# A one-core hybrid DeltaNet and Hyena trunk: three seams between its stages rearranged together

## The chip, the cores and the metric

The kernel runs on one core of one Trainium2 chip. The time is that of the whole program on the device, in microseconds. TensorE is called PE, its weight load PEld, VectorE DVE, ScalarE ACT, GpSimd POOL and SyncE SP.

## The reference

One layer over a sequence of 2048 tokens of width 1024, and 256 context tokens:

```python
mod_x = silu(c) @ w_mod + b_mod                      # shift, scale and gate, each 1024 wide
hx = rmsnorm(x, norm_g) * (1.0 + sc_x) + sh_x
px = hx @ w_in                                       # q, k, v, z_a, betas, decays, hy_v, hy_x1, hy_x2, z_b, g_a, g_b
ox, _ = deltanet(px, lp, rows, GRID_W, ctx_states)   # chunked gated delta rule, forward and backward, 8 heads
yx = hyena(px, lp, rows, GRID_W)                     # two long convolutions by Fourier transform
x = x + gt_x * ((sigmoid(g_a) * (ox @ w_pa) + sigmoid(g_b) * (yx @ w_pb)) @ w_out)
out = rmsnorm(x, final_g)
```

The sum of the two delta directions is normed per head (mean of squares of 128 values) before it is gated and multiplied by `w_pa`. All is fp32.

## The kernel before

Five stages run one after the other, each in a block of its own: `modulate`, `project`, `delta`, `hyena`, `merge`. Each stage has a `Kit` that holds its on-chip buffers and semaphores. At its end all engines meet at a barrier and the semaphores are cleared (L159), so a stage's last DMA that must have landed holds back the next stage. Two outer kits, `shared` and `tail`, keep what several stages use. Within a stage each engine has its own written order of instructions, and waits on counting semaphores. SP issues most DMAs, POOL some from a queue of its own, ACT a few.

**modulate.** A tile is 128 tokens of 1024 values; there are 18, the first two context. POOL loads a tile into one of four slots `xin`; ACT squares and sums it (`square`), DVE makes the mean, ACT the root, DVE inverts and scales it into `xs`, PE turns it in eight transposes (`tile`), and ACT and DVE move half each out of PSUM (`move`). Between tiles PE multiplies the condition by `w_mod`, in 12 pieces of 256 columns (`piece`), of which the first 8 (shift and scale) are needed before anything can be shaped, and the last 4 are the gate row. The slots `wm` of the first 8 pieces lie in `hB`, where the last eight tiles go. So `HEAD_TILES` (10) tiles run first with a piece each, then the windows 0 (context), 1 and 2 are shaped (`shape`: scale and shift), then the other eight tiles with the gate's pieces through one buffer `wmg`, then windows 3 and 4. A window of the sequence is 512 tokens. The sums S1 to S4 are operands of a seven-product scheme in `project`: those of the first half of the sequence are made between the last eight tiles, those of the second half after the last shaping, and all seven operands of the second half are stored to `comb` by SP, which `modulate` waits for. `gate_products` multiplies each shaped window by the 32 columns of betas and decays, `keep` copies them out, `gate_turns` turns them. POOL loads the first two blocks of `w_in` into `wt` after 15 tiles.

**project.** 40 steps, each a pair of 128-column blocks of `w_in` for one half of the sequence, in seven products (P1 to P7). SP's queue stores the results to scratch tensors: `store(s - 2, 1)` and `store(s - 1, 0)` in turn `s`.

**delta.** 72 pairs of heads. For each, SP loads `rows`, `kq`, `nv`, `ttc` and `tnc` for both directions, ten DMAs, into a ring of `DEPTH` = 6; `sc` holds all scalars. POOL subtracts (`differences`, L1704) and places blocks (L1713), ACT takes exponentials, DVE weighs, PE multiplies (L1939, L1882, and others).

**hyena.** Eight steps `t` (four blocks of channels, two orders). In each, PE, ACT and DVE make spectra and products, and SP stores the eight parts of the inverse to `bounce_i` (L2172), waits for all, and reads them back turned (L2178); PE then makes the eight output banks `O` (L2521), and DVE empties them (`outputs`). In the last step this is followed by turning the result to channels (`results`), and by the store of `yT` (L2183), for which the stage waits. POOL's queue also loads what the merge needs: its weights `w_pb` and rows in `merge_weights`, and in `merge_operands` `w_pa` (4 MB, L2331) when the last T bank is filled and the delta's `o` (two loads of 1 MB, L2335) when the last M bank is.

**merge.** Eight windows of 256 tokens. In each, POOL adds the directions of `o` (L2781), ACT squares, DVE reduces, inverts and scales, per half (`norm_half`); PE turns `o` (L2898), DVE weighs with `z_a` (L2840). Behind it, for the window before, come eight products of `w_pa` and `w_pb` (L2908, L2912), DVE's gates (L2850), POOL's mix (L2790), `w_out` (L2926) and the final norm. The engines' order per window puts both `norm_half` ahead of the gates on DVE.

## Time and profile before

| | |
|---|---|
| Runs | 4446.98 us median of 3 (4445.2 to 4453.29) |
| The profiled execution | 4446.54 us, its span 4444.8 us |
| Busy share | PE 95%, DVE 55%, POOL 39%, ACT 28% |
| Mean granted TensorE clock | 0.974 |
| HBM traffic | 405 MB read, 218 MB written, 140 GB/s over the span |

Times in the rows are microseconds from the span's start. A row of the timeline gives the start and the length of a run of like instructions, the engine (SPq is SP's queue of DMA issues), the source line, output and inputs, the number of instructions, and in brackets how long the engine had been idle before it and what ended that.

### The profile page before, as it was taken

What the parts mean: (1) busy time and instruction counts of PE and PEld (TensorE: products, weight loads), DVE (VectorE), ACT (ScalarE), POOL (GpSimd) and SP (SyncE); (2) the same over time, 40 slices, a digit from 0 to 9 for tenths busy, and PEclk for the clock granted to TensorE, in tenths of its full rate; (3) what the DMA queues carried; (4) which work ended last, traced back from release to release, by engine and by line L of the source; (5) the groups of instructions that cost most, each with busy time, mean ns of one, the idle gap of its engine ahead of it and who ended that gap; (6) DMA issues with size and microseconds to landing.
All of it is one profiled execution on the core that took longest, in us unless ns stands there. A gap on an engine that the chain in (4) does not pass through costs nothing. (4 is left out here: it accounts for less than half of the span.)

```text
span 4444.8 us, 72318 instructions
## 1 busy us (share of the span) xinstructions
PE 4225.1 (95%) x28915; PEld 2587.0 (58%) x28915; DVE 2437.7 (55%) x3482; ACT 1233.2 (28%) x2592; POOL 1752.8 (39%) x1487
## 2 busy tenths in 40 slices
PE   5899999999999999999979999989999996999998
PEld 3466544444445544444437888856565654767776
DVE  4555755542446668896616666657676763222221
ACT  4122121111222211111115555555555551000000
POOL 1222233332333343433339989845444451111111
PEclk7999999999999999999989999999999997999999
DMA  6323222223242342425337788567767677223320
GB/s 232 103 74 98 76 94 82 76 95 115 82 154 85 107 117 81 123 76 166 108 128 210 217 261 248 165 178 229 223 195 230 213 246 273 76 76 115 111 76 29
DMA packets 481064, 627.05 MB, mean 141 GB/s; under 512 B 120928, under 2 KB 379944, under 8 KB 470124
## 3 DMA queue, kind: packets, MB, share of 16 engines
q1 hardware_dynamic: 431596, 484.22, 35.9%
q0 software_dynamic: 28560, 113.25, 7.9%
q10 hardware_dynamic: 20592, 25.16, 1.7%
q8 instruction: 222, 3.64, 0.3%
q14 instruction: 94, 0.77, 0.1%
HBM read 405.01 MB, written 217.53 MB: 140 GB/s over the span
## 5 line engine op out<-in xcount | busy, mean ns | idle before, releaser
L1458 PE MATMUL proj_b<-shared_S,proj_tw 128*128 128x512 f32 x1920 | 850.8, 595 | 0.0
L1458 PEld LDWEIGHTS proj_b<-shared_S,proj_tw 128*128 128x128 f32 x1920 | 361.7, 191 | 433.9 <-issue 433.5
L1458 PE MATMUL proj_b<-shared_A,shared_wt 128*128 128x512 f32 x1280 | 577.4, 594 | 13.0 <-PEq L159 12.3
L820 POOL TENSOR_TENSOR proj_tw<-shared_wt 128x512 f32<-128x512 f32 x80 | 109.9, 1374 | 921.3 <-PE proj_b L1458 838.6
L1458 PEld LDWEIGHTS proj_b<-shared_A,shared_wt 128*128 128x128 f32 x1280 | 243.8, 191 | 317.5 <-issue 317.1
L1458 PE MATMUL proj_b<-shared_A,proj_tw 128*128 128x512 f32 x640 | 289.4, 595 | 3.2 <-DVE proj_u L1125 3.2
L1458 PE MATMUL proj_b<-shared_S,shared_wt 128*128 128x512 f32 x640 | 290.9, 597 | 0.0
L1023 ACT ACTIVATE proj_v<-proj_b 128x512 f32<-128x512 f32 x80 | 47.8, 597 | 634.9 <-PE proj_b L1458 634.9
L1840 DVE SCALAR_TENSOR_TENSOR delta_la<-delta_kkq,delta_sc,delta_wm 128x256 f32<-128x256 f32 (+1 forms) x288 | 121.6, 464 | 173.3 <-PE delta_kkq L1939 173.2
L1458 PEld LDWEIGHTS proj_b<-shared_A,proj_tw 128*128 128x128 f32 x640 | 122.2, 191 | 157.6 <-issue 152.6
L1704 POOL TENSOR_SCALAR delta_ex<-delta_rows,delta_sc 128x128 f32<-128x128 f32 x288 | 203.5, 721 | 22.5 <-DMA delta_tnc<-scratch_Tn 22.5
L1120 DVE TENSOR_TENSOR proj_u<-proj_b,proj_u 128x512 f32<-128x512 f32 x80 | 55.2, 690 | 277.0 <-PE proj_b L1458 276.8
L2926 PE MATMUL mrg_b<-mrg_w_o,tail_u 128*128 128x512 f32 x448 | 198.3, 594 | 6.7 <-POOL tail_u L2790 4.3
L834 POOL TENSOR_TENSOR proj_tw<-shared_wt,proj_tw 128x512 f32<-128x512 f32 x80 | 116.7, 1458 | 199.9 <-PE proj_b L1458 199.8
L1719 POOL TENSOR_SCALAR delta_kg<-delta_nv,delta_sc 128x128 f32<-128x128 f32 x288 | 187.9, 668 | 10.1 <-PE delta_kv L1956 10.1
L1136 DVE TENSOR_TENSOR proj_rawx<-proj_b,proj_u 128x512 f32<-128x512 f32 x144 | 97.5, 683 | 172.0 <-PE proj_b L1458 171.9
L1458 PEld LDWEIGHTS proj_b<-shared_S,shared_wt 128*128 128x128 f32 x640 | 117.1, 191 | 128.2 <-issue 127.8
L1014 ACT ACTIVATE proj_u<-proj_b 128x512 f32<-128x512 f32 x80 | 47.6, 596 | 517.0 <-PE proj_b L1458 494.7
L2416 DVE TENSOR_TENSOR fft_second<-fft_b,fft_second 128x512 f32<-128x512 f32 x256 | 159.5, 682 | 54.6 <-PE fft_b L2544 47.1
L2310 POOL TENSOR_TENSOR tail_u<-tail_u,fft_ga 128x4096 f32<-128x4096 f32 x8 | 71.5, 8935 | 266.7 <-DMA fft_ga<-scratch_hy 137.9
L844 POOL TENSOR_TENSOR proj_u<-proj_u,proj_v 128x512 f32<-128x512 f32 x80 | 136.0, 1700 | 103.0 <-ACT proj_v L1023 102.9
L806 POOL DMA_DIRECT2D shared_wt<-in_w_in_dram x78 | 70.5, 904 | 265.2 <-PE proj_b L1458 265.2
(333 smaller groups left out, 8583.1 us busy)
## 6 DMA issues: line engine op xcount, KB each, us to landing
shared_wt<-in_w_in_dram POOLq DMA_DIRECT2D x80, 1024.0 KB, 6.0
delta_nv<-scratch_NV SPq DMA_DIRECT2D x144, 256.0 KB, 4.1
delta_kq<-scratch_KQ SPq DMA_DIRECT2D x128, 256.0 KB, 4.3
scratch_bounce_f<-tail_first SPq DMA_DIRECT2D x128, 256.0 KB, 4.4
tail_yf<-scratch_bounce_f SPq DMA_DIRECT2D x32, 1024.0 KB, 7.3
scratch_bounce_i<-fft_yi SPq DMA_DIRECT2D x64, 512.0 KB, 3.4
fft_second<-scratch_bounce_i SPq DMA_DIRECT2D x32, 1024.0 KB, 8.6
scratch_hy<-proj_tok SPq DMA_DIRECT2D x48, 512.0 KB, 2.6
```

The costliest lines, as they stand in the source:

```text
L806: pool.dma_start(wt[:, s % 2, :, :], wv[:, :, col:col + 2 * P]).then_inc(w_in[s % 2], 16)
L820: pool.tensor_tensor(T3, w[:, hi, second], w[:, lo, second], ALU.subtract).then_inc(combined, 1)
L834: pool.tensor_tensor(T4, w[:, hi, first], T2, ALU.subtract).then_inc(combined, 1)
L844: pool.tensor_tensor(u4[:, :], u2[:, :], v5[:, :], ALU.add).then_inc(fourth, 1)
L1136: dve.tensor_tensor(out, rows(bank[:, :]), rows(addend[:, :]), ALU.add).then_inc(dve_read, 1)
L1458: last = pe.matmul(bank[:, :], weights[:, k, :], aa[operand][:, k, :], start=(k == 0), stop=(k == KH - 1))
L1704: last = pool.tensor_scalar(ex[:, n % 2, d, g, :], rows[:, n % DEPTH, d, g, :], scalar(n, d, g, Q_NGC), 0.0, ALU.add, ALU.min)
L1719: last = pool.tensor_scalar(kg[:, n % SYS, d, g, :], nv[:, n % DEPTH, d, g, 0, :], scalar(n, d, g, Q_BKL), None, ALU.mult)
L1840: last = dve.scalar_tensor_tensor(out=la[:, n % SYS, d, g, parts, :], in0=b_kkq[g][:, 2 * P * d:2 * P * (d + 1)].rearrange("p (a t) -> p a ...
L2310: pool.tensor_tensor(data, data, ga[:, :, :, :], ALU.mult).then_inc(gated, 1)
L2416: dve.tensor_tensor(dst[h % 2][:, i, :], bank(kind, t, 2 * h + i)[:, :], xs[h % 2][:, i, :], ALU.mult).then_inc(emptied["dve"], 1)
L2926: last = pe.matmul(out_banks(h)[b][:, :], mt[:, k, h * P:(h + 1) * P], w_o(k)[:, 512 * b:512 * b + 512], start=(k == 0), stop=(k == KT - 1))
```

## The change

It has three parts, joined by one shared space.

**A shared space.** A new outer kit, `bridge`, keeps a region of 7360 values per partition and three semaphores through the whole program. `modulate` puts its short-lived buffers there, `project` its scratch region, `delta` its scalars and the first two of the six ring entries, and `hyena` and `merge` their `yf` and `hs`.

**modulate.** `wm` now lies over S1 to S4, the four gate pieces have a buffer each, and all 18 tiles run first, with a piece at every second one. After that all five windows are shaped in a row; of windows 3 and 4 ACT shapes five rows of eight and DVE three. The sums of the first half stand between windows 2 and 3, in one group. `keep` comes after all shaping, and POOL loads `wt` after all tiles.

**delta's operands ahead.** SP loads `sc2` and the first two pairs in the last step but one turn of `project`, before it stores that turn's results. `delta` waits for these at its start, SP goes on with pair 2, the clearing of the state moves from POOL to DVE, and ACT makes one exponential at once.

**The merge's first norm.** In the hyena's last step POOL loads `o` first, adds both halves, and loads `w_pa` after output bank 1 is filled. ACT and DVE make the norm of window 0 before the last outputs; `epsq` and `dng` are loaded for it by SP. The wait for the store of `yT` moves from the hyena's end to the merge, before SP's load of `yb`.

The diff, cut to its core:

```diff
+        wm = [aa[x][:, :, :].rearrange("p k t -> p (k t)").rearrange("p (k n) -> p k n", k=KT) for x in ("S1", "S2", "S3", "S4")]
+        wg = [wmg[:, :, :], pieces(xin[:, 2:4, :]), pieces(xin[:, 0:2, :]), pieces(xs[:, :, :])]
+        def split(w):
+            return KH if w < HEAD else KH - 1
...
+                sp.dma_start(wg[0], gates[:, 0, :, :]).then_inc(wg_in[0], 16)
+                sp.wait_ge(scaled, NCH - 2)
+                sp.dma_start(wg[1], gates[:, 1, :, :]).then_inc(wg_in[1], 16)
+                sp.wait_ge(scaled, NCH)
+                sp.dma_start(wg[2], gates[:, 2, :, :]).then_inc(wg_in[2], 16)
+                sp.wait_ge(turned, NCH)
+                sp.dma_start(wg[3], gates[:, 3, :, :]).then_inc(wg_in[3], 16)
...
-                    if i == NCH - NX:
-                        for s in range(2):
+                pool.wait_ge(products, HEAD_PIECES)
+                for s in range(2):
...
-                tiles(0, HEAD_TILES)
-                for w in range(HEAD):
+                tiles(0, NCH)
+                for w in range(5):
                     shape(w)
-                for w in range(2):
-                    keep(w)
-                tiles(HEAD_TILES, NCH)
-                for w in range(HEAD, 5):
-                    shape(w)
-                for w in range(2, 5):
+                for w in range(5):
                     keep(w)
...
+                def sums(w):
+                    for who in ("act", "dve"):
+                        dve.wait_ge(shaped[who], w)
+                    if w > HEAD:
+                        dve.wait_ge(summed, 3)
+                        dve.wait_ge(differed, 1)
+                        dve.wait_ge(z_done, 3)
...
+                tiles(0, NCH, keep_vectors)
                 vectors()
                 for w in range(HEAD):
                     shape(w)
-                tiles(HEAD_TILES, NCH, sums)
+                sums(3)
                 for w in range(HEAD, 5):
                     shape(w)
...
+                sums(5)
...
-                for i in range(HEAD_TILES):
+                for i in range(NCH):
                     tile(i)
-                    if i >= 4 and i % 2 == 0:
-                        vectors(i // 2 - 2)
-                    if i >= 2:
-                        piece(i - 2)
+                    if i >= 6 and i % 4 == 2:
+                        vectors(i // 4 - 1)
+                    if i >= 2 and i % 2 == 1:
+                        piece(i // 2 - 1)
...
+def load_pair(sp, T, ring, n, landed):
+    chunks, j = pair_of(n)
+    for d in range(2):
+        c, heads = chunks[d], slice(2 * j, 2 * j + 2)
+        parts = slice(0, parts_of(n))
...
+                def pairs_ahead():
+                    last = first_step(1, "k") + H // 2 - 1
+                    sp.wait_ge(inv_out, 64 * NPIECE)
+                    sp.wait_ge(sc_out, 48)
+                    for m in range(2):
+                        sp.wait_ge(tok_out[m], 16 * tok_dmas[NSTEP])
+                        for s in (last - 1, last):
+                            sp.wait_ge(chan_out[s % 2][m], 16 * chan_stores(s))
+                    sp.dma_start(S["bridge"][:, 0:SC_SIZE], T["sc2"].rearrange("p c h d q -> p (c h d q)")).then_inc(S["sc_in"], 16)
+                    for n in range(AHEAD):
+                        load_pair(sp, T, ring_entry(S["bridge"], SC_SIZE + n * RING_SIZE), n, S["pair_in"][n])
                 for s in range(NSTEP + 2):
+                    if s == NSTEP - 1:
+                        pairs_ahead()
                     store(s - 2, 1)
...
-                sp.dma_start(sc[:, :, :, :, :], T["sc2"]).then_inc(loaded, 16)
                 sp.dma_start(tri[:, :, :], T["tri"]).then_inc(loaded, 16)
                 sp.dma_start(blocks[:, :], T["blocks"]).then_inc(loaded, 16)
-                sp.wait_ge(cleared, 1)
-                for n in range(NPAIR):
-                    chunks, j = pair_of(n)
+                for n in range(AHEAD, NPAIR):
...
-                pool.memset(S[:, :, :, :], 0.0).then_inc(cleared, 1)
-                pool.wait_ge(loaded, 48)
+                pool.wait_ge(L["sc_in"], 16)
...
+                act.activation(warm[:, :], sc[:, 0, 0, 0, 0:1], ACT.Exp, scale=0.0)
...
+                dve.memset(S[:, :, :, :], 0.0).then_inc(cleared, 1)
...
+                    if t == STEPS - 1:
+                        epsq, _, _, dng = tail_norm(L)
+                        sp.dma_start(epsq, T["epsq"]).then_inc(L["small"], 16)
...
-                sp.dma_start(T["yT"][2 * NCB - 2:2 * NCB, :, :].rearrange("h p t -> p h t"), yt).then_inc(y_stored, 16)
-                sp.wait_ge(y_stored, 16 * NCB)
+                sp.dma_start(T["yT"][2 * NCB - 2:2 * NCB, :, :].rearrange("h p t -> p h t"), yt).then_inc(L["y_out"], 16)
...
-                    ready(pool, "T", last, N2 - 1)
-                    pool.dma_start(tail_w_a(L), T["w_pa"][0].rearrange("(k p) n -> p k n", p=P)).then_inc(L["w_a_in"], 16)
                     ready(pool, "M", last, N2 - 1)
...
+                    o = tail_o(L)
+                    pool.wait_ge(L["o_in"], 32)
+                    for h in range(2):
+                        pool.tensor_tensor(o[:, h, 0, :], o[:, h, 0, :], o[:, h, 1, :], ALU.add).then_inc(L["summed"], 1)
+                    ready(pool, "O", last, 1)
+                    pool.dma_start(tail_w_a(L), T["w_pa"][0].rearrange("(k p) n -> p k n", p=P)).then_inc(L["w_a_in"], 16)
...
+                def first_norms():
+                    o, (epsq, ms, sd, _) = tail_o(L), tail_norm(L)
...
+                    for h in range(2):
+                        dve.wait_ge(L["rooted"], h + 1)
+                        dve.reciprocal(sd[:, h, :], sd[:, h, :]).then_inc(L["inverted"], 1)
+                        dve.wait_ge(L["inverted"], h + 1)
+                        dve.tensor_tensor(heads(o[:, h, 0, :]), heads(o[:, h, 0, :]), sd[:, h, :].unsqueeze(2).broadcast_to([P, H, P]), ALU.mult).then_inc(L["scaled"], 1)
                 for t in range(STEPS + 1):
+                    if t == STEPS:
+                        first_norms()
...
+                        if off == 0:
+                            sp.wait_ge(L["y_out"], 16)
...
+        B = {"bridge": kit.sb("region", P, SC_SIZE + AHEAD * RING_SIZE), "sc_in": kit.sem("sc_in"), "pair_in": [kit.sem(f"pair_in{n}") for n in range(AHEAD)]}
```

## Rows read from the trace of the kernel before

**Rows 1.** The page, part 1: busy time of each engine.
```profile
PE 4225.1 (95%) x28915; PEld 2587.0 (58%) x28915; DVE 2437.7 (55%) x3482; ACT 1233.2 (28%) x2592; POOL 1752.8 (39%) x1487
```

**Rows 2.** Windows: length, busy us (instructions) of each engine, granted clock, DMA share, GB/s.
```profile
4.00:48.00 44.00, 27.45 (x227) 19.37 (x230) 19.01 (x49) 19.25 (x42) 5.71 (x10) 0.92 1.07 369
3678.00:3697.00 19.00, 1.45 (x24) 0.18 (x16) 0.32 (x1) 1.08 (x2) 0.63 (x1) 0.63 0.98 380
```

**Rows 3.** Timeline of the first 130 us.
```profile
47.51 1.58 PE L485 MATMUL mod_b<-mod_hB,mod_scond 128*32 128x256 f32 x16 [2.42 <-DMA mod_hB<-in_w_mod_dram]
...
52.35 2.07 ACT L330 ACTIVATE shared_hc<-mod_hA,mod_mod,mod_gsc 128x256 f32<-128x256 f32 x4 [6.62 <-DVE mod_gsc L413]
...
54.33 5.74 ACT L330 ACTIVATE shared_A<-mod_hA,mod_mod,mod_gsc 128x512 f32<-128x512 f32 x8
...
55.47 1.91 DVE L423 TENSOR_SCALAR mod_hA<-mod_hA,mod_gsc,mod_mod 128x512 f32<-128x512 f32 x4
...
60.48 3.64 PE L516 MATMUL mod_b<-shared_A,mod_wbg 128*32 128x512 f32 x16 [4.06 <-ACT mod_zs L337]
...
106.16 2.76 SPq L268 DMA_DIRECT2D scratch_comb<-mod_hB  x3
...
112.90 2.29 DVE L456 TENSOR_TENSOR mod_hA<-mod_hB,mod_hA 128x2048 f32<-128x2048 f32 x1
...
129.46 5.56 PE L1458 MATMUL proj_b<-shared_A,shared_wt 128*128 128x512 f32 x8 [12.30 <-PEq L159]
```

**Rows 4.** Timeline of the seam between projection and delta.
```profile
2307.69 1.80 POOL L1697 MEMSET delta_S<- 128x2048 f32 x1 [14.01 <-POOLq L159]
...
2309.52 0.33 SPq L1688 DMA_DIRECT2D delta_rows<-scratch_gcT  x1
...
2314.70 0.47 SPq L1688 DMA_DIRECT2D delta_rows<-scratch_gcT  x1
...
2318.24 2.80 POOL L1704 TENSOR_SCALAR delta_ex<-delta_rows,delta_sc 128x128 f32<-128x128 f32 x4 [8.74 <-DMA delta_tnc<-scratch_Tn]
```

**Rows 5.** Timeline of the hyena's last gap.
```profile
3675.35 0.95 POOL L2331 DMA_DIRECT2D tail_first<-in_w_pa_dram  x1
...
3677.23 1.41 POOL L2335 DMA_DIRECT2D tail_yf<-scratch_o  x2 [0.93 <-PE fft_b L2544]
...
3696.78 2.04 SPq L2178 DMA_DIRECT2D fft_second<-scratch_bounce_i  x4
3701.60 16.74 PE L2521 MATMUL fft_b<-fft_second,tail_ia 128*128 128x256 f32 x64 [22.14 <-DMA fft_second<-scratch_bounce_i]
3705.49 0.69 DVE L2396 TENSOR_TENSOR fft_ga<-fft_b,fft_ga 128x512 f32<-128x512 f32 x1 [27.18 <-PE fft_b L2521]
...
3724.74 0.39 SPq L2183 DMA_DIRECT2D scratch_yT<-fft_ga  x1
```

**Rows 6.** Tile `fft_yi`, 3640 to 3700: landing of its eight bounce stores.
```profile
DMA to landing us min/median/max: 2.9/3.8/16.0
```

**Rows 7.** Timeline of the merge's start.
```profile
3732.74 4.64 POOL L2781 TENSOR_TENSOR tail_yf<-tail_yf 128x1024 f32<-128x1024 f32 x2 [54.10 <-SPq L2709]
...
3733.72 0.38 SPq L2728 DMA_DIRECT2D tail_ia<-scratch_yT  x1
...
3739.66 1.94 PE L2898 MATMUL mrg_b<-tail_ident,tail_yf 128*128 128x128 f32 x8 [16.09 <-DVE tail_yf L2828]
...
3747.51 5.62 PE L2908 MATMUL mrg_b<-tail_aT,tail_first 128*128 128x256 f32 x16 [1.59 <-DVE tail_aT L2840]
...
3769.07 2.06 DVE L2850 TENSOR_TENSOR mrg_gg<-mrg_b,mrg_gg 128x512 f32<-128x512 f32 x3
...
3778.01 3.62 PE L2908 MATMUL mrg_b<-tail_aT,tail_first 128*128 128x256 f32 x16
```

**Rows 8.** `scratch_yT`, 3700 to 3735: landing of the store (6.4) and of `yb` (5.4).
```profile
DMA to landing us min/median/max: 5.4/5.9/6.4
```

**Rows 9.** Timeline of the end.
```profile
4439.35 0.39 SPq L2740 DMA_DIRECT2D out_dram<-tail_u  x1
```

More of the change, by code:

```diff
@@ L1601 @@
 SYS = 3
-def pair_of(n):
-    s, j = divmod(n, PAIRS)
-    back = NCTX - 1 - s if s < NCTX else NCH - 1 - (s - NCTX)
-    return (s, back), j
 def level_blocks(d, h):
@@ L1641, in delta @@
         loaded, cleared = kit.sem("loaded"), kit.sem("cleared")
-        landed = [kit.sem(f"landed{i}") for i in range(DEPTH)]
+        landed = [L["pair_in"][i] if i < AHEAD else kit.sem(f"landed{i}") for i in range(DEPTH)]
         stored = [kit.sem(f"stored{i}") for i in range(2)]
@@ L2674, in merge @@
         ident = L["ident"]
-        dng, eps = kit.sb("dng", P, 1), kit.sb("eps", P, 1)
-        epsq = kit.sb("epsq", P, NCH, H)
+        epsq, _, _, dng = tail_norm(L)
+        eps = kit.sb("eps", P, 1)
         ms, sd, rs = (kit.sb(n, P, 2, H) for n in ("ms", "sd", "rs"))
@@ L2710, in _ @@
                 sp.sem_inc(za_in[0], 16)
-                sp.dma_start(epsq[:, :, :], T["epsq"]).then_inc(small, 16)
-                with nc.allow_non_contiguous_dma(reason="a vector into a column"):
-                    sp.dma_start(dng[:, :], T["dn_norm_g"][0].rearrange("(p a) -> p a", a=1)).then_inc(small, 16)
                 sp.sem_inc(stored, 16)
@@ L2816, in norm_half @@
                     def norm_half(h):
-                        if not front:
+                        if not front or off == 0:
                             return
```

228 lines of the change are left out of this document (131 added, 97 removed).

## The prediction

> **What bounds the kernel now.** I read the page first. TensorE is busy 95% of the span [rows 1], so time can come back only from the 5% in which it idles. Then I asked for the windows of 100 to 500 us over the whole span: the idle time stands in three places, the first 129 us, the seam of projection and delta near 2305 us, and the stretch from 3680 to 3750 us, the last gap of the hyena and the start of the merge. For each I took the timeline in order of time, the waits, and the windows with the DMA rate. The change touches exactly these three.
>
> In the first place the transfers are saturated, not the engines: from 4 to 48 us they moved 369 GB/s while PE was busy 27 of 44 us [rows 2]. At the second seam nothing computes while the first pair's loads are issued and land: POOL is free at 2307.69 (its first work is a memset) and its first subtraction starts at 2318.24 [rows 4]. In the third, DMA moved 380 GB/s for 19 us while PE was busy 1.45 of them [rows 2]: `w_pa`, `o` and the last bounce store drain together, 7.3 MB, and only then does SP read the bounce back at 3696.78 [rows 5]. After that come the wait for the store of `yT` and a norm before PE turns anything.
>
> **Front.** Removed: the split of the 18 tiles into 10 and 8 with the shaping of three windows between them. All tiles now come first, a piece of `w_mod` with every second one, from four slots laid over S1 to S4. The bytes needed before the last tile and piece: 18 tiles of 0.52 MB, 8 pieces of 1.05 MB, and one gate piece and `wbg` queued beside them, 19.0 MB. At 369 GB/s [rows 2] from 4 us on that is 51.5 us, so 55.5. Before, from the last piece's products (47.51) to the first shaping (52.35) were 4.8 us [rows 3]; so shaping starts at 60, called T. Per tile the transfers need 2.8 us. The engines need less: for the ten tiles before, ACT was busy 19.3 us and PE, pieces included, 27.5 [rows 2], so DMA paces it. If handshakes do (before, a tile with its piece took 4.35 us; let one without still need 3.4, an estimate between this and the 2.8), T is 4 + 61.2 + 4.8 = 70; with the gate piece not in the way, T is 57. I take 60, since the row at 369 GB/s is the nearest.
>
> From T: ACT shapes window 0 (2.07 for four) and windows 1 and 2 (5.74 for eight) [rows 3], to T+7.8; DVE is quicker, 1.91 for four. Then DVE's four sums of 2.28 each [rows 3], to T+17.1, and its three rows of windows 3 and 4, 6 x 0.48, to T+20.0. ACT has ten of 0.72 there and is done at T+15. Then the seven stores to `comb` begin, as at 106.16 before, and the projection begins 23.3 us later, at 129.46 [rows 3], because the stores' 7.3 MB and the closing of the block take that long. Late next: the copies `keep` now stand behind all shaping on ACT, and the second sums wait for the third gate product. That product comes at about T+24 (two of 3.64 us at the low clock [rows 3] and their copies), so the sums end 3.5 us later, at T+32.6. The first three stores alone fill the DMA until T+28 and S1 and S3 until T+34, so this is hidden; without that cover it costs 3.5. The projection starts at T+43.3 = 103.3, for 129.46: **-26.1** (bounds -16 and -29). The loads of `wt` move behind all tile loads on POOL's queue and land by about T+10, free; DMA idles from there to T+20.
>
> **Projection to delta.** SP issues `sc2` and two pairs (21 DMAs) in step 39's turn. A pair takes 5.2 us of SP's queue (2309.52 to 2314.70 [rows 4]), so 10.9 us. Behind them wait the last stores of `gb`, whose buffers are needed two steps on; 40 steps fill 129.46 to 2307.69, 54 us each in the mean, so I count nothing; uncovered it is 10.9. At the seam POOL's subtraction may start at once at 2307.7 instead of 2318.24: **-10.5**. The memset goes to DVE (POOL's took 1.80 [rows 4]; from half to twice that there, an estimate), behind DVE's two others, and is hidden until about 2311.2, when POOL's four subtractions (2.80 [rows 4]) and the exponential behind them are done. `tri` and `blocks` are now the first loads; if they land as late as pair 0's last (some 4 us from its issue, 2318.24 less 2314.2), POOL's placements move from 2310.5 to 2312.4, which costs up to 1.9. Against that ACT's table load is made ahead. Pair 2 is issued from 2308.6 instead of 2314.70, 6 us earlier, while POOL wants it 10.5 earlier, about 2320; with landing it is there by 2318. I take -10.0, bounds -8 and -12.
>
> **Last gap and merge.** (a) `w_pa`, 4.2 MB, leaves the queue at 3675.35 and is issued only after the second output bank. What remains at 3677.8 is `o` (2.1 MB) and two bounce stores (1.05 MB): 3.15 MB at 380 GB/s [rows 2] is 8.3 us, so 3686 instead of 3696.78 [rows 5]: I take 3685.5, as other stores there landed in 2.9 to 3.8 us and only this one in 16.0 [rows 6]. PE's outputs begin 11.3 us earlier, at 3690.3 (bounds: 12.4 if the store lands at once in 3.8, 0 if something else holds it). `w_pa` goes out at 3697.2, behind POOL's adds, beside the end of the read-back and needs 11 us at that rate; PE asks for it at 3715.4.
>
> The Trainium skill ("DMA: Bandwidth & Descriptors", section "Queues, rings and completion order") says that a DMA engine takes turns between the queue rows it has work for, packet by packet. With equal shares of bytes the store would last at most twice 3.8 us whatever the other queue holds, also in the changed kernel, and the gap would shrink by 8.7 instead of 11.3; the 16.0 of [rows 6] shows that the shares are not equal here, so the trace decides.
>
> (b) The norm in the gap: `o` is there at 3686, POOL adds two halves (4.64 us [rows 7] for both), ACT squares, DVE reduces, inverts and scales. In the merge the first half took 3732.74 to 3739.66 [rows 7], 6.9 us; the second ends some 3.5 behind it: about 10.4 us, to 3696.4. DVE's first output bank is full at 3705.49 - 11.3 = 3694.2, so DVE is 2.2 us late. It needs 1.4 us a bank (two instructions of 0.69) where PE brings one in 2.1 in the mean (16.74 for eight) [rows 5], so it has caught up before the last. Cost 0 (up to 3 if `o` lands late). `epsq` and `dng` on SP fall into an idle stretch.
>
> (c) The `yT` store goes out at 3724.74 - 11.3 = 3713.4; the hyena no longer waits for its 6.4 us [rows 8]. Before, the merge began 8.0 us after the issue [rows 5, 7], so now 1.6 after it plus the issue: 3715.4. PE turns and DVE weighs, twice: 7.85 us before, from 3739.66 to 3747.51 [rows 7], of which some 0.7 waited for the second half's norm; with 7.1 the first product could start at 3722.5 instead of 3747.51. (d) But what is late next is SP: it waits for the store's landing, 3719.8, before it issues `yb`, `gg`, `w_out` and the next window's `o`. That queue set the next norm: from the issue of `yb`, 3733.72, to DVE's first gate, ending at 3769.8, are 36.0 us, DMA-bound, and the fifth product (3778.01) had 8 us to spare [rows 7]. Now the gate ends at 3719.8 + 36.0 = 3755.8, while PE would have been ready at 3722.5 + 30.5 = 3753.0: it waits 2.8 us. The fifth product starts at 3755.9 for 3778.01: **-22.1**, whatever clock PE has on the way. `yb` itself lands after 5.4 us [rows 8], in time.
>
> **End.** One more kit is closed. From the last store's issue at 4439.35 to 4444.8 [rows 9] are 5.4 us with a landing and two closings; one closing after the 6.4 us of `yT` took 1.6. **+0.7** (0 to 1.6).
>
> **Sum.** -26.1 - 10.0 - 22.1 + 0.7 = -57.5. Against the profiled execution's 4446.5 that is 4389.0; the runs' median is 0.4 higher, which I leave.
>
> **Rivals.**
> *The front is paced by handshakes*, not bytes: T = 70, the projection at 113, 4399. For it: 4.35 us a tile is near the bytes' own 4.25, so the row does not show how short the chain can be; against: no engine was busy two thirds of the time. 20%.
> *The last gap does not shrink*, because the store is held by `o` or by packet sharing: 11.3 are lost, 4400. For it: `o` stays in the gap; against: its bytes are a third. This is also the case in which moving `w_pa` does not do what it says. 14%.
> *`w_pa` comes late*: at the pace of a 0.5 MB store (3.8 us [rows 6]) 4 MB take 30 us, PE waits from 3715.4 to 3727, and of this 8.8 stay after (d): 4398. For it: nothing shows that transfer alone; against: the same queue was the largest part of 380 GB/s. 6%.
> *More comes back*: T = 57 (3), the delta at its bound (2), the store at once (1), the merge's loads 2 us quicker: 4381. 10%.
> *Slower*: TensorE's granted clock. It averaged 0.974. If the denser schedule made the clock fall there, each hundredth costs some 42 us of the 4225 busy ones [rows 1]; from 1.4 hundredths on the kernel is slower, 4456 at 1.6. Nothing in the trace hints at it: gaps lower the clock here (0.63 in the gap [rows 2]), work does not. 2%.
>
> **Numbers.** My own case, 4382 to 4396, 48%. The range runs from the bound "more" to beyond the front and the gap rivals: 4376 to 4406; outside it are both rivals at once and the slow one. A change of under 0.2%, 9 us, cannot be told from none; faster 0.97, same 0.01, slower 0.02.
>
> **What would show it.** The first product of the projection at 103 (a step of 3 tells T). POOL's first subtraction in the delta within a microsecond of its start. The read-back of the bounce 6 to 7 us after the last store instead of 16. PE's turn right at the start of the merge, then one wait of about 3 us for a gate before the fifth product. Wrong would be: DMA below 350 GB/s in the first 50 us, the gap still 22 us, or a PE wait for `w_pa` at the merge's start.

## The result, and the profile after

The changed kernel takes 4398.44 us (median of 4 runs, 4395.3 to 4402.8), the kernel before 4447.57 (4 runs). The ratio is 0.9893, with a 95% interval of 0.9881 to 0.9906: faster by 49 us where 57.5 were forecast, inside the range of 4376 to 4406. The profiled execution has a span of 4396.3 us for 4444.8, so 48.5 less. TensorE's mean granted clock is 0.980 for 0.974.

The two traces, cut at landmarks that both have:

| stretch | before | after | difference | forecast |
|---|---|---|---|---|
| start to the projection's first product | 129.46 | 110.44 | -19.0 | -26.1 |
| to DVE's first memset of the delta | 2178.4 | 2177.3 | -1.1 | 0 |
| to POOL's first subtraction | 10.4 | -0.35 | -10.7 | -10.0 |
| to the hyena's last inverse bank (TensorE, 16 products in a row) | 1359.0 | 1357.2 | -1.8 | 0 |
| to the issue of the last `yT` store | 47.5 | 39.4 | -8.1 | -11.3 |
| to the fifth product of the merge | 53.3 | 43.3 | -10.0 | -10.8 |
| to the end | 666.8 | 669.0 | +2.2 | +0.7 |

The stretches that the change leaves alone also differ between executions. Over the 12 kernels below, the projection's ran from 2173.9 to 2180.1 us, the fourth from 1354.4 to 1364.0 and the last from 667.2 to 669.1. A single execution therefore says nothing about a whole time within 5 us or so, and the experiments are read by stretch.

The page of the changed kernel, part 1, against [rows 1]:
```profile
PE 4219.2 (96%) x28915; PEld 2583.1 (59%) x28915; DVE 2441.7 (56%) x3481; ACT 1234.5 (28%) x2595; POOL 1750.6 (40%) x1486
```
TensorE does the same work in 5.9 us less busy time; the other 42.6 us were idle time.

Timeline of the front, changed kernel, against [rows 3]: the issues of two late tiles, the arrival of the last (its square on ACT), the last piece's products, the first shaping, the first store of `comb`, the projection:
```profile
40.09 0.53 POOL L297 DMA_DIRECT2D mod_xin<-in_x_dram  x1 [4.65 <-DVE bridge_region L384]
...
50.01 0.53 POOL L297 DMA_DIRECT2D mod_xin<-in_x_dram  x1 [1.20 <-DVE bridge_region L384]
...
58.20 1.06 ACT L313 ACTIVATE bridge_region<-mod_xin 128x1024 f32<-128x1024 f32 x1 [0.54 <-DMA mod_xin<-in_x_dram]
...
63.91 1.07 PE L481 MATMUL mod_b<-shared_S,mod_scond 128*32 128x256 f32 x16
...
67.46 2.07 ACT L339 ACTIVATE shared_hc<-mod_hA,mod_mod,mod_gsc 128x256 f32<-128x256 f32 x4 [2.84 <-DVE mod_gsc L415]
...
87.05 2.75 SPq L279 DMA_DIRECT2D scratch_comb<-mod_hB  x3
...
110.44 2.05 PE L1506 MATMUL proj_b<-shared_A,shared_wt 128*128 128x512 f32 x2 [10.80 <-PEq L159]
```
T is 67.5 and not 60; from T on the stores start 19.6 later (20.0 was forecast) and the projection 43.0 later (43.3). The bracket on the POOL rows is the point: POOL had the next load ready and waited for DVE to be done with the slot. Windows of the same stretch:
```profile
4.00:24.00 20.00, 8.28 (x37) 6.79 (x41) 8.28 (x26) 10.47 (x23) 2.99 (x5) 1.00 1.06 373
24.00:44.00 20.00, 14.85 (x122) 10.07 (x115) 10.92 (x27) 11.67 (x28) 3.26 (x7) 0.85 1.00 353
...
40.00:44.00 4.00, 4.00 (x26) 2.40 (x27) 2.31 (x6) 2.15 (x7) 1.06 (x2) 0.50 0.88 294
44.00:48.00 4.00, 3.97 (x40) 3.15 (x38) 2.96 (x9) 2.71 (x6) 0.53 (x1) 0.90 0.82 278
```
The last column falls from 373 and 353 GB/s to 294 and 278 between 40 and 48 us, where TensorE is full, for four of these us at a granted clock of 0.50, its lower level of 1.2 GHz. There the transfers wait for the engines; in the next 8 us they are back at 327 and 388 GB/s.

Timeline of the second seam, against [rows 4]:
```profile
2287.43 2.80 POOL L1733 TENSOR_SCALAR delta_ex<-bridge_region 128x128 f32<-128x128 f32 x4 [14.13 <-POOLq L159]
...
2288.86 1.30 PE L1974 MATMUL delta_kkq<-bridge_region 128*32 128x128 f32 x32 [7.75 <-DVE delta_kkq L1851]
2289.22 1.76 DVE L1852 MEMSET delta_S<- 128x2048 f32 x1 [0.42 <-issue]
...
2293.54 0.44 PE L1915 MATMUL delta_lev<-bridge_region,delta_la 32*32 32x32 f32 x16 [3.38 <-DVE delta_la L1874]
```
The subtraction starts with the block instead of 10.4 us into it, and `delta_lev` follows it by 6.1 us for 6.9 before. The memset of `S` lies beside POOL's subtractions, as counted.

Timeline of the last gap and the merge's start, against [rows 5, 7]:
```profile
3637.55 10.87 SPq L2212 DMA_DIRECT2D scratch_bounce_i<-fft_yi  x4
...
3644.61 1.48 POOL L2383 DMA_DIRECT2D bridge_region<-scratch_o  x2 [3.15 <-PE fft_b L2615]
...
3654.54 4.64 POOL L2387 TENSOR_TENSOR bridge_region<-bridge_region 128x1024 f32<-128x1024 f32 x2 [8.45 <-DMA bridge_region<-scratch_o]
3656.08 1.97 SPq L2218 DMA_DIRECT2D fft_second<-scratch_bounce_i  x4
...
3684.06 0.39 SPq L2223 DMA_DIRECT2D scratch_yT<-fft_ga  x1
3685.86 0.06 DVE L2887 MEMSET mrg_eps<- 128x1 f32 x1 [1.87 <-PEq L159]
3686.89 1.94 PE L2985 MATMUL mrg_b<-tail_ident,bridge_region 128*128 128x128 f32 x8 [4.00 <-DVEq L2893]
...
3691.22 0.38 SPq L2806 DMA_DIRECT2D tail_ia<-scratch_yT  x1
...
3694.12 5.14 PE L2995 MATMUL mrg_b<-tail_aT,tail_first 128*128 128x256 f32 x16 [1.58 <-DVE tail_aT L2925]
...
3727.32 5.41 PE L2995 MATMUL mrg_b<-tail_aT,tail_first 128*128 128x256 f32 x16 [2.71 <-DVE mrg_gg L2935]
```
The last of the four stores goes out at the end of its row, at 3648.05, and the read-back 8.0 us behind it, for 16.1 before and 4.8 forecast. `o` is there at 3654.5: the store, issued behind it, lands behind it. The last row shows the forecast wait before the fifth product, 2.7 us for 2.8.

### The profile page after: what moved, and what is told of

Same layout as the page of the kernel before. It is cut to its first block and busy times, and to the rows that moved or that the text cites. A ratio compares the mean times of both kernels' runs of the same rounds, so it can differ in the third digit from the quotient of the medians.

```text
span 4396.3 us, 72326 instructions
## 1 busy us (share of the span) xinstructions
PE 4219.2 (96%) x28915; PEld 2583.1 (59%) x28915; DVE 2441.7 (56%) x3481; ACT 1234.5 (28%) x2595; POOL 1750.6 (40%) x1486
## 3 DMA queue, kind: packets, MB, share of 16 engines
q1 hardware_dynamic: 431596, 484.22, 36.4%
## 5 line engine op out<-in xcount | busy, mean ns | idle before, releaser
L1506 PE MATMUL proj_b<-shared_A,shared_wt 128*128 128x512 f32 x1280 | 578.5, 595 | 11.4 <-PEq L159 10.8
L1874 DVE SCALAR_TENSOR_TENSOR delta_la<-delta_kkq,bridge_region,delta_wm 128x256 f32<-128x256 f32 (+1 forms) x288 | 121.5, 463 | 170.7 <-PE delta_kkq L1974 170.5
L2353 POOL TENSOR_TENSOR fft_acc<-fft_acc,fft_yi 128x512 f32<-128x512 f32 x120 | 153.1, 1276 | 38.3 <-ACT fft_yi L2257 27.7
L2841 ACT ACTIVATE tail_fan<-tail_u 128x1024 f32<-128x1024 f32 x16 | 16.9, 1057 | 530.5 <-POOL tail_u L2882 530.5
```

What stands on the lines that cost most here:

```text
L1506: last = pe.matmul(bank[:, :], weights[:, k, :], aa[operand][:, k, :], start=(k == 0), stop=(k == KH - 1))
L1874: last = dve.scalar_tensor_tensor(out=la[:, n % SYS, d, g, parts, :], in0=b_kkq[g][:, 2 * P * d:2 * P * (d + 1)].rearrange("p (a t) -> p a ...
L2353: pool.tensor_tensor(acc[:, :], acc[:, :], sq[:, n % 2, :], ALU.add).then_inc(added, 1)
```

## Experiments

All are edits of the changed kernel. T is the start of the shaping, "behind the last bank" counts from the last inverse bank of the hyena.

**Front: what sets T.** Three kernels.

e1, each piece a tile earlier on TensorE:
```diff
-                    if i >= 2 and i % 2 == 1:
+                    if i >= 2 and i % 2 == 0:
                         piece(i // 2 - 1)
-                    q, rest = divmod(n - 7, 4)
+                    q, rest = divmod(n - 6, 4)
```


> The changed kernel with each of the first eight pieces multiplied one tile earlier (the last one stands between the last two tiles on TensorE instead of behind the last). Theory A, the time T at which shaping starts is the landing of the last tile (58.2) plus the chain behind it, 9.3 us, in which the last piece's products are a link of 1.9 us: T falls from 67.5 to about 65.6 and the projection starts at 108.5 instead of 110.4; the whole about 2 us shorter. Rival B, the last piece waits for its own transfer or for the handshakes of the tiles, so its place on TensorE changes nothing: T stays at 67.5 within 0.5. DMA up to 56 us is the same in both.

e2, six slots:
```diff
-        NX, NW = 4, 4
+        NX, NW = 6, 4
+        spare = aa["A22"][:, :, :].rearrange("p k t -> p (k t)")
+        x_slot = lambda i: xin[:, i % NX, :] if i % NX < 4 else spare[:, (i % NX - 4) * D:(i % NX - 3) * D]
...
-                    pool.dma_start(xin[:, i % NX, :], source(i))
+                    pool.dma_start(x_slot(i), source(i))
```


> The changed kernel with six slots for the tiles of x instead of four (the two more lie in an operand that is free until the shaping). Theory B, the slots pace the front (a tile's load is issued only when the tile four before it is scaled): the last issue moves from 50.0 to about 44, DMA holds 370 GB/s from 40 to 52 us instead of 278 to 330, the 19.0 MB are in by 55.4, and T falls by 2.5 us or more, to 65 or less. Theory A, the bytes pace it as they are: the loads are issued earlier but land at the same times, T stays between 66.5 and 67.5.

e3, the gate piece behind the tiles:
```diff
-                sp.dma_start(wg[0], gates[:, 0, :, :]).then_inc(wg_in[0], 16)
                 sp.wait_ge(scaled, NCH - 2)
+                sp.dma_start(wg[0], gates[:, 0, :, :]).then_inc(wg_in[0], 16)
```


> The changed kernel with the first gate piece (1.05 MB) issued only when sixteen tiles are scaled, so behind the tiles instead of among them. Theory A, bytes: the last tiles land 1.05 MB / 370 GB/s = 2.8 us earlier and T falls to about 64.7, the projection starts 2.8 us earlier. Theory B, slots and handshakes: T stays at 67.5 within 0.5.

| | last tile issued | squared | last piece | T | square to T |
|---|---|---|---|---|---|
| changed kernel | 50.0 | 58.2 | 63.9 | 67.5 | 9.3 |
| e1 | 52.8 | 58.5 | 61.8 | 65.3 | 6.9 |
| e2 | 40.3 | 51.1 | 55.8 | 59.4 | 8.3 |
| e3 | 49.8 | 57.3 | 63.6 | 67.2 | 9.9 |

The eight other kernels here that have this front unchanged up to T (e4 to e11) put T at 66.0 to 69.0, and the last square at 57.5 to 59.2. e2 lies far outside: T falls by 8.1 us, and 7.1 of them are the last tile's earlier square. Its timeline and windows:
```profile
40.31 0.53 POOL L299 DMA_DIRECT2D shared_A<-in_x_dram  x1 [5.79 <-DVE bridge_region L386]
...
59.39 2.07 ACT L341 ACTIVATE shared_hc<-mod_hA,mod_mod,mod_gsc 128x256 f32<-128x256 f32 x4 [2.84 <-DVE mod_gsc L417]
...
102.44 6.08 PE L1508 MATMUL proj_b<-shared_A,shared_wt 128*128 128x512 f32 x8 [9.76 <-PEq L159]
```
```profile
24.00:44.00 20.00, 14.62 (x120) 10.77 (x116) 12.21 (x30) 11.44 (x28) 3.18 (x6) 0.79 1.06 376
44.00:56.00 12.00, 10.85 (x108) 7.61 (x104) 8.79 (x22) 7.70 (x20) 0.00 (x0) 0.92 1.10 340
```
The transfers hold 376 GB/s for 353 in the second 20 us. e3 moves 1.05 MB out of the way; its last square is at 57.3, 0.2 us below the range of the eight others and 0.9 before the changed kernel's, not 2.8, and T stays at 67.2. The two together settle it: four slots paced the end of the front (theory B), not the bytes. With six the bytes are the next limit: PE waited once for a piece of `w_mod`, 3.6 us at 36.4, which it never did in the changed kernel, and the busy share of the DMA engines was 1.06 from 24 to 44 us and 1.10 from 44 to 56 (1.00 from 24 to 44 in the changed kernel). e1 takes 2.4 us out of the chain behind the last tile; 6.9 lies below the 8.3 to 10.8 of the eleven kernels with the old order (e12, below, has 6.9 too), so that link was real as well, though T alone would not show it against its scatter.

**Last gap: what holds the last store.** e4, `w_pa` behind `o`:
```diff
+                    pool.dma_start(tail_w_a(L), T["w_pa"][0].rearrange("(k p) n -> p k n", p=P)).then_inc(L["w_a_in"], 16)
                     o = tail_o(L)
                     pool.wait_ge(L["o_in"], 32)
...
-                    ready(pool, "O", last, 1)
-                    pool.dma_start(tail_w_a(L), T["w_pa"][0].rearrange("(k p) n -> p k n", p=P)).then_inc(L["w_a_in"], 16)
```


> The changed kernel with w_pa (4.2 MB) issued right behind the loads of o in the last gap, not behind the second output bank. Theory A, the last bounce store is done only when nearly all that is in flight has drained (7.3 MB at 380 GB/s): read-back 16 us behind the last store as before the change, the gap of TensorE 22.1 us instead of 14.1, the whole 8 us longer, less what the merge gets back. Theory B, queues take turns and only what lies ahead in the other queue counts, or the store goes at a share of its own: read-back stays 8.0 behind the store, the gap 14.1, the whole the same within 1 us.

e8, `o` issued when the stores have landed:
```diff
                     ready(pool, "M", last, N2 - 1)
+                    for i in range(2):
+                        pool.wait_ge(i_written[i], 64 * STEPS)
...
                     if t and t % 2 == 0:
                         empty_out(t // 2 - 1)
+                    if t == STEPS:
+                        first_norms()
```
(the call of `first_norms` moves there on ACT and DVE, and POOL issues `w_pa` ahead of its adds)

> The changed kernel with the loads of o issued when the last bounce stores have landed, beside the read-back, w_pa behind the second output bank as now ahead of the adds, and the first norm behind the last output banks on ACT and DVE instead of ahead of them. Theory A (what holds the last store is only what is in flight with it): the store lands in 3.8 us, the read-back is issued about 4.5 behind it instead of 8.0 and the gap of TensorE shrinks from 14.1 to 10.5 to 12, less what o takes from the read-back; the norm ends near the yT store and the fifth product comes 2 to 3 us earlier. Rival B (the wait moves to the read-back, whose first quarter now shares with o): the gap stays at 13 to 14, and the late norm makes the merge start later than now.

e9, half of `o` on either side of the stores:
```diff
+                    for h, sem in enumerate((L["o_in"], L["o_in1"])):
+                        if h:
+                            for i in range(2):
+                                pool.wait_ge(i_written[i], 64 * STEPS)
...
+                        pool.dma_start(o[:, h, :, :], src).then_inc(sem, 16)
...
+                        first_norms(0)
...
+                        first_norms(1)
```
(`first_norms(0)` stands where `first_norms()` stood, `first_norms(1)` behind `empty_out`)

> The changed kernel with only the first half of o (1.05 MB) loaded in the last gap and the second when the last bounce stores have landed; the first half's norm stays ahead of the last output banks, the second's goes behind them, where only TensorE's second turn needs it. Theory A (the last store lands with what is in flight beside it): with half of o the read-back is issued about 5.5 behind the last store, between the 8.0 with all of o and the 2.9 with none; the gap of TensorE is 11.6 instead of 14.1, the yT store and the fifth product come 2.5 us earlier (36.9 and 80.2 behind the last forward product bank instead of 39.4 and 82.7). Rival B (the second half is late now): the gap shrinks as much, but the second turn waits and the fifth product stays where it is, 82.7 behind.

The read-back is issued as soon as the last store has landed. What that did to the gap, in us (the last two columns from the last bank on):

| kernel | in flight beside the store | read-back behind the store | TensorE's gap | `yT` store | fifth product |
|---|---|---|---|---|---|
| e8 | nothing | 3.0 | 9.0 | 35.8 | 82.3 |
| e9 | half of `o` | 5.7 | 12.0 | 36.4 | 80.7 |
| changed kernel | `o` | 8.0 | 14.1 | 39.4 | 82.7 |
| e4 | `o`, then `w_pa` | 13.6 | 21.5 | 46.2 | 89.5 |
| before | `w_pa`, then `o` | 16.1 | 22.1 | 47.5 | 100.7 |

```profile
3655.46 2.19 SPq L2218 DMA_DIRECT2D fft_second<-scratch_bounce_i  x4
3655.97 1.48 POOL L2385 DMA_DIRECT2D bridge_region<-scratch_o  x2 [9.26 <-DMA scratch_bounce_i<-fft_yi]
3660.31 16.18 PE L2594 MATMUL fft_b<-fft_second,tail_ia 128*128 128x256 f32 x64 [9.03 <-DMA fft_second<-scratch_bounce_i]
...
3672.91 5.10 POOL L2391 TENSOR_TENSOR bridge_region<-bridge_region 128x1024 f32<-128x1024 f32 x2 [5.57 <-DMA bridge_region<-scratch_o]
...
3684.84 0.39 SPq L2223 DMA_DIRECT2D scratch_yT<-fft_ga  x1
3692.76 1.94 PE L2987 MATMUL mrg_b<-tail_ident,bridge_region 128*128 128x128 f32 x8 [9.11 <-DVEq L2895]
```
These rows of e8 show why the shortest gap is not the best kernel. The gap is 5.1 us shorter, but `o` is loaded beside the read-back and is there only at 3672.9, and TensorE's first turn comes 7.9 us behind the `yT` store instead of 2.8. Rival B was wrong on the gap and right on what follows; theory A, with a fifth product 2 to 3 us earlier, missed (0.4). In e9 only the second half is late:
```profile
3656.36 2.37 SPq L2218 DMA_DIRECT2D fft_second<-scratch_bounce_i  x4
...
3661.52 15.75 PE L2597 MATMUL fft_b<-fft_second,tail_ia 128*128 128x256 f32 x64 [12.03 <-DMA fft_second<-scratch_bounce_i]
```
The fifth product comes 80.7 us behind the last bank, 2.0 us earlier and near the 80.2 of theory A. e4 undoes the move of `w_pa` in its queue: 6.8 us of the 8.1 come back. So theory A holds for it, on the stretch: its whole time, 4400.75 us, is only 2.3 above the changed kernel's and not 8, because its projection was 3.4 us shorter and its last stretch 1.7, for which "End" below has the reason.

**Second seam.** e5 loads the scalars and the first two pairs in the delta:
```diff
-                    if s == NSTEP - 1:
-                        pairs_ahead()
...
+                sp.dma_start(L["bridge"][:, 0:SC_SIZE], T["sc2"].rearrange("p c h d q -> p (c h d q)")).then_inc(L["sc_in"], 16)
...
+                for n in range(AHEAD):
+                    load_pair(sp, T, ring[n], n, landed[n])
```


> The changed kernel with the part at the second seam alone undone: the scalars and the first two pairs are loaded at the start of the delta instead of in the last step of the projection. Theory A (the seam is worth its wait and the 21 DMAs ahead cost the projection nothing): POOL's first subtraction starts about 10.5 us later after the end of the projection (6.3 now), TensorE's first wait in the delta grows from 7.7 to 16 or more, the projection keeps its 2170.7 us. Rival B (the DMAs ahead hold SP and the last stores of the projection back): the projection is 2 us or more shorter than now, and the net worth of the part is under 8.


```profile
2290.69 1.03 DVE L1852 MEMSET delta_kkq<- 128x512 f32 x2 [5.96 <-PEq L159]
...
2300.48 1.30 PE L1975 MATMUL delta_kkq<-bridge_region 128*32 128x128 f32 x32 [16.48 <-DMA bridge_region<-scratch_Tn]
2300.53 2.80 POOL L1734 TENSOR_SCALAR delta_ex<-bridge_region 128x128 f32<-128x128 f32 x4 [24.34 <-DMA bridge_region<-scratch_Tn]
```
The subtraction comes 9.8 us behind DVE's memset, the wait of 16.5 us is back, and the projection takes 2178.7 us, in the middle of the 2173.9 to 2180.1 of the others. So the seam is worth 10.2 us (-0.35 against 9.84), and no cost of the 21 DMAs can be seen; one of 2 us, as rival B has it, would be lost in that scatter of 6. The whole was 4418.2 us, 20 over the changed kernel, and the rest lies in stretches that the edit leaves alone: 1.5 in the front, 1.4 in the projection and 6.8 between the subtraction and the last bank. Of these 6.8 the delta has 1.0: from its first subtraction to its last product into `delta_ks` it took 575.3 us, where all the other kernels have 573.8 to 577.2.

**Merge.** e6, the wait for the store of `yT` back at the hyena's end:
```diff
                 sp.dma_start(T["yT"][2 * NCB - 2:2 * NCB, :, :].rearrange("h p t -> p h t"), yt).then_inc(L["y_out"], 16)
+                sp.wait_ge(L["y_out"], 16)
```


> The changed kernel with SP waiting for the store of yT at the end of the hyena, as before the change. Theory A (behind the seam the fifth product is set by SP's loads, which wait for that store anyway, so the early start of TensorE is worth only part of the 6.2): first product 6.2 us later behind the store's issue (16.3 instead of 10.1), fifth product 16.3 + 30.5 = 46.8 behind it instead of 43.3, so 3.5 later, without a wait for a gate. Rival B (everything behind the seam follows its start): 6.2 later.

The first product came 16.1 us behind the store's issue and the fifth 46.4, without a wait for a gate: 3.1 us later, not 6.1. Theory A. The other half of the early start is spent waiting for the gate. By the sixth product e6 is only 1.3 us behind, 53.3 for 52.0, since its fifth ran at the higher clock ("End" below).

e7, the gate loads ahead of SP's wait, `yb` behind it:
```diff
-                        if off == 0:
-                            sp.wait_ge(L["y_out"], 16)
...
                             sp.dma_start(gg[:, s, :, c, :], T[name][:, :, cols].rearrange("k p t -> p k t")).then_inc(g_in[s], 16)
+                        if off == 0:
+                            sp.wait_ge(L["y_out"], 16)
+                            sp.dma_start(yb[:, s, :, :], T["yT"][:, :, cols].rearrange("k p t -> p k t")).then_inc(y_in[s], 16)
```


> The changed kernel with SP issuing the two gate loads (2.1 MB) at the merge's start, ahead of its wait for the store of yT, and yb, w_out and the next o behind it as now. Theory A (the loads behind that wait set the next norm, so the bytes taken out of that queue bring it forward): o lands up to 5.7 us earlier, DVE's first gate too, TensorE's wait of 2.7 us before the fifth product goes, and that product starts 40.6 us behind the issue of the yT store instead of 43.3. Rival B (the chain of the next norm or yb holds it): the wait of 2.7 us stays, or one for yb in the first product takes its place.


```profile
3696.93 0.37 SPq L2810 DMA_DIRECT2D tail_ia<-scratch_yT  x1
...
3707.17 1.99 PE L3001 MATMUL mrg_b<-tail_ia,tail_fa 128*128 128x256 f32 x8 [2.71 <-DMA tail_ia<-scratch_yT]
```
The fifth product starts 43.1 us behind the store, as before the edit. The wait for the gate is gone, and one of 2.7 us for `yb` stands in the first product, ahead of its `w_pb` part: rival B. That both waits are 2.71 us is not shown to be more than chance. `yb` now took 10.2 us to land, with the gates in flight, where 5.4 had been [rows 8].

**From T to the projection.** e10, the first gate copy on ACT ahead of the last two windows; e11, DVE shaping all windows before it sums:
```diff
-                for w in range(5):
+                for w in range(3):
                     shape(w)
-                for w in range(5):
+                keep(0)
+                for w in range(3, 5):
+                    shape(w)
+                for w in range(1, 5):
                     keep(w)
```


> The changed kernel with the copy of the first gate product on ACT ahead of the shaping of the last two windows instead of behind it. Theory A (as the prediction has it: the late second sums are hidden by the stores' bytes): the second and third gate product and the last two stores of comb come 2 to 3 us earlier (28 to 29.5 behind T instead of 31.1), but the projection still starts 43.0 behind T, within 0.5. Rival B (the sums are on the path): it starts 2 to 3 us earlier behind T.


```diff
-                for w in range(HEAD):
-                    shape(w)
-                sums(3)
-                for w in range(HEAD, 5):
+                for w in range(5):
                     shape(w)
+                sums(3)
                 sums(5)
```


> The changed kernel with DVE shaping all five windows ahead of its eight sums, not four sums in between. Theory A (from T on the end of the block is set by the bytes of seven stores, which begin when DVE's last shaping is done): the first store goes out 15.5 behind T, when ACT is done, instead of 19.6, and the projection starts 39 to 40 behind T instead of 43.0. Rival B (the sums, or the third gate product, set the last stores): the last two stores go out at 31 behind T as now, and the projection starts 42 to 43 behind it.

In e10 the last two stores went out 28.7 us behind T, 2.4 earlier than in the changed kernel, and the projection still began 42.8 behind T (43.0). The late sums are hidden by the stores' bytes, as the prediction had it. Rows of e11:
```profile
82.93 3.90 SPq L279 DMA_DIRECT2D scratch_comb<-mod_hB  x3
...
99.71 1.20 SPq L286 DMA_DIRECT2D scratch_comb<-mod_hA  x2
...
108.11 4.37 PE L1504 MATMUL proj_b<-shared_A,shared_wt 128*128 128x512 f32 x6 [7.32 <-PEq L159]
```
Here T is 68.14: the first store goes out at T + 14.8, the last two at T + 31.6, and the projection starts at T + 40.0, 3.0 us earlier. That is the start of theory A, at its upper edge, with the last two stores where rival B had them (31.1 in the changed kernel). The projection now follows these two by 8.4 us instead of 11.9; what sets them is not shown.

**Together.** e12 has e1, e2, e9, e10 and e11 in one kernel.

> The changed kernel with the pieces a tile earlier, six slots, DVE shaping first, the first gate copy early, and half of o in the gap. If the parts add up: T at 58 (8.0 us from the slots, part of the 2.2 from the piece), the projection at T + 39.5 = 97 to 98 instead of 110.4, the gap 2.5 us shorter: 15 to 16 us faster than the changed kernel, 4383 us, ratio to the kernel before 0.9855. If the slots and the earlier piece take the same wait away and the sums are on the path: 9 to 10 us, 4389, ratio 0.987. If the bytes before T bind now, T stays at 59.4 and the rest holds: 4384.

It takes 4384.85 us (median of 4 runs, 4382.0 to 4386.4), against 4447.09 for the kernel before (7 runs): 0.9859, 95% interval 0.9843 to 0.9875, which lies wholly below that of the changed kernel. T is 58.0, the projection starts at 96.6, TensorE's gap is 11.7 us and the fifth product comes 80.5 us behind the last bank. By these stretches it gains 13.9 + 2.2 = 16.1 us over the changed kernel; the medians differ by 13.6. The profiled spans differ by 16.4, because of the unchanged stretches the projection was 3.4 us shorter, the one to the last bank 4.8 longer and the last one 1.8 shorter. T fell by 1.4 from e2's, so the slots and the earlier piece add up in part.

The whole times of the others, one run each, lie close together and rank them only where the effect is large: e1 4401.8 us, e2 4387.6, e3 4401.3, e6 4396.3, e7 4401.6, e8 4400.6, e9 4397.4, e10 4399.6, e11 4393.1. In e1, for one, the projection was 2.8 us and the stretch to the last bank 5.2 us longer than in the changed kernel, which hid the 2.2 us of its front.

## Why the prediction was right, and where it was off

**Busy time.** "Time can come back only from the 5%" was not quite so: 5.9 of the 48.5 us are busy time, with the mean granted clock 0.006 higher. By the prediction's 42 us a hundredth that would have been 25 us. The mean clock also counts stretches in which TensorE idles at a low one (0.63 in the gap [rows 2]), so it does not price busy time.

**Front, -19.0 for -26.1.** The part behind T was right to 0.3 us, and e10 confirms that the late sums cost nothing. The step that failed is "T is 60", and it failed in both of its terms. For the pace I compared busy times ("the engines need less [...] so DMA paces it"). What counts is the way round of one slot: load, square, root, scale, and only then the next load. The last tile was issued at 50.0, 37.7 us behind the fifth, so 2.9 us a tile, and it was squared at 58.2 where I had the bytes in by 55.5. For the end I took the 4.8 us from the last piece's products to the shaping and let them start with the last byte. But the last tile's own norm, its turn and then the piece stand between: 9.3 us from its square to T. With six slots (e2) T is 59.4 and the projection starts at 102.4, for 60 and 103.3 forecast. That is no proof of my sum, since there the last square was at 51.1 and the chain 8.3: the terms were off in opposite directions. The 7.5 us by which T came late are 2.7 in the pace and 4.5 in the chain, and 0.3 of rounding down to 60. The rival "paced by handshakes" named the right cause at 20%, with 3.4 us a tile for 2.9 and T = 70.

**Projection to delta, -10.7 for -10.0.** Right in mechanism and size; e5 gives 10.2 for the prefetch alone. `delta_lev` gained 0.8 us more: ACT's first exponential came 2.8 us behind the start of the subtraction for 4.2, with no table load (1.28 us) in between. POOL waited 0.18 us for `blocks`, of the 1.9 counted for it at most.

**Last gap, -8.1 for -11.3.** The mechanism was right: the store's landing hangs on what is in flight (e4). The size was off by 3.2, because I let `o` off too lightly. I added up the bytes left (8.3 us at 380 GB/s) from 3677.8, the issue of `o`, and had the store in by then. In the changed kernel it took 11.5 us from the issue of `o` (3644.6) to the read-back, at 320 GB/s from 3647 on, and the store came in last. The table gives the price: half of `o` costs 2.7 us, all of it 5.0. The upper bound of 12.4 (the store at once in 3.8) needed `o` out of the gap; e8 shows 3.0 us for the store then, and a gap 13.1 us shorter than before.

The rule that I weighed against it is from the Trainium skill, "DMA: Bandwidth & Descriptors", section "Queues, rings and completion order": a DMA engine switches between the queue rows it has work for after each packet. Read as equal shares of bytes, that puts the store at no more than twice its own 3.0 us. The trace disagrees with that reading: 8.0, 13.6 and 16.1 us, growing with what the other queue holds. That the 8.7 us by which it would have let the gap shrink (8.5 by the rows, 16.1 less twice 3.8) are closer to the 8.1 than mine is chance.

**The norm in the gap costs nothing.** Right. From the start of the outputs to the `yT` store are 23.1 us in both kernels, and DVE's first bank is taken 3.9 us behind TensorE's start in both.

**Merge, -10.0 for -10.8.** Right, link by link: the block starts 1.8 us behind the `yT` store's issue (1.6), `yb` goes out 7.2 behind it (6.4), the fifth product follows `yb` by 36.1 (36.1), and the new wait is 2.7 (2.8). What is missing is 0.8 us in the landing of the store with the closing of the wait. `w_pa` was there in time; no wait on it is in the trace.

**End, +2.2 for +0.7.** From the last store's issue (4390.41) to the end are 5.9 us, for 5.4: +0.5, as forecast. The rest is the fifth product itself and what follows it: to the sixth it is 8.7 us, for 6.9 before. Rows and windows of that product, in the changed kernel and in e1:
```profile
3727.32 5.41 PE L2995 MATMUL mrg_b<-tail_aT,tail_first 128*128 128x256 f32 x16 [2.71 <-DVE mrg_gg L2935]
3727.32:3732.56 5.24, 5.24 (x16) 4.29 (x17) 3.05 (x5) 0.00 (x0) 2.83 (x4) 0.67 0.89 319
3732.43 3.72 PE L2995 MATMUL mrg_b<-tail_aT,tail_first 128*128 128x256 f32 x16 [1.68 <-DVE mrg_gg L2935]
3732.43:3735.99 3.56, 3.56 (x16) 3.15 (x17) 3.06 (x5) 0.00 (x0) 2.81 (x4) 1.00 1.08 377
```
After the wait of 2.7 us the granted clock was at its lower level for most of the product (0.67 over it). So it was in e3, e5, e10 and e11, which also waited 2.71 us, and their last stretch took 669.0 or 669.1 us. In the other eight (a wait of 1.5 to 1.7 us or none) the clock was 1.00 there and the stretch 667.2 to 667.4. Among them is e7, which ran its first products like the five (0.84 for 0.85 from 10 to 20 us behind the `yT` store) but had no such wait. So the lower clock went with the wait in every kernel; that the wait causes it is not shown by an edit of its own. The prediction had the wait, 2.8 us, and gave it no price beyond itself ("whatever clock PE has on the way"); in the changed kernel 1.8 us more went with it.

**The chances.** Neither rival came as written. The front lost 7.1 of the 10 us that "handshakes" gave it, the gap 3.2 of the 11.3 of the other, and seam and merge met their terms. Each of the rivals was priced as all or nothing; in the trace both came in part, and the time, 4398, is where either alone would have put it.

## What to carry to other kernels

A load loop with few slots is paced by one slot's way round (issue, landing, every engine until the slot is free), and an engine's busy share doesn't show it: look for the idle time in front of the issuing engine, and try more slots before taking bytes away. A block's end is the last arrival plus the whole chain of that last item, not the last link that was seen before. And when a transfer on the path lands late, price what is in flight beside it piece by piece, then follow the transfer that was moved: `o` out of the gap shortened it by 5 us and gave nearly all of it back as a late norm; half of `o` gave back less than it gained. And look at the granted clock of the instructions behind a wait of TensorE: here 1.8 us more were lost there than the 2.7 of the wait.

## What the runs showed of the hardware

- The read-back of the bounce, which waits for the last 0.5 MB store, went 3.0 us behind it when nothing was in flight on the other queue, 5.7 with 1.05 MB in flight there, 8.0 with 2.1 MB and 13.6 with 6.3 MB: some 2.5 us for each of the first two MB. The order in that queue matters too, 13.6 with `w_pa` last (e4) and 16.1 with it first (the kernel before, in which all loads were also issued earlier against the store, and which differs in more than this).
- `yb` took 5.4 us when issued first, and 10.2 us with 2.1 MB of gates ahead of it and `w_out` behind it (e7).
- TensorE's wait of 2.71 us before the fifth product of the merge was followed by a granted clock of 0.67 over that product, 5.4 us long, in all five kernels that had it; with 1.5 to 1.7 us or no wait (nine kernels) it was 1.00 and 3.6 to 3.7 us.
- The same instructions of the projection took 2173.9 to 2180.1 us in different executions, TensorE over 99% busy: a scatter larger than most single edits here are worth. Part of it is the clock: in e4, e11 and e12, the shortest, the mean granted clock of the stretch was 1.00 and TensorE busy for 2162.8 us, in e1, e3 and e9, the longest, 0.99 and 2168.1 to 2168.6.
